# A tile of tokens ranked ahead of the others, and the order of gathers, gates and kept GELUs in a product-key expert layer on Trainium2

## The reference

```python
def peer_layer(h, w_q, sub_keys, u_tab, v_tab):      # T = 512, D = 1024
    q = (hf @ w_q).reshape(T, PEER_HEADS, 2, PEER_DQ // 2)          # 8 heads, 2 halves of 128
    s = jnp.einsum('thpd,hpnd->thpn', q, sub_keys)                  # 128 keys per half
    sc, idx = lax.top_k(s, PEER_TOPK)                               # 16 of 128
    cand = (sc[:, :, 0, :, None] + sc[:, :, 1, None, :])            # 16 x 16 sums
    cidx = (idx[:, :, 0, :, None] * PEER_NKEYS + idx[:, :, 1, None, :])
    top_sc, pos = lax.top_k(cand, PEER_TOPK)                        # 16 of 256
    eidx = jnp.take_along_axis(cidx, pos, axis=-1)                  # of 16384 experts
    gate = jax.nn.softmax(top_sc, axis=-1)
    act = gelu(einsum('thkd,td->thk', u_tab[eidx], h))
    return einsum('thk,thkd->td', gate * act, v_tab[eidx])
```

## Time and profile before

| | |
|---|---|
| median of 3 runs | 3418.14 us |
| the profiled execution | 3415.01 us, its span 3413.2 us |
| TensorE busy | 3213.3 us (94%), granted clock 0.981 as a mean |
| VectorE, ScalarE, GpSimd busy | 2236.4, 1360.5, 1723.1 us |
| DMA | 587.55 MB, mean 172 GB/s |
| up stage with its gate runs | about 820 to 1481 us of the span |
| down stage | about 1481 to 2063 us |

### The profile page before, as it was taken

How to read it: one execution, slowest core, us unless ns; L and a number is a source line. 1 busy time by engine, 2 the same in 40 slices (tenths; PEclk the granted TensorE clock), 3 DMA queues, 4 the chain that set the end, 5 groups by cost and what they waited for, 6 DMA issues and landing times.

```text
span 3413.2 us, 46478 instructions
## 1 busy us (share of the span) xinstructions
PE 3213.3 (94%) x16195; PEld 2774.4 (81%) x16195; DVE 2236.4 (66%) x4113; ACT 1360.5 (40%) x1999; POOL 1723.1 (50%) x922
## 2 busy tenths in 40 slices
PE   6999999989999999979999999898999999899998
PEld 4787787779999999979999998756888886478886
DVE  5787898769968677646666645286854332857553
ACT  4555432333454544434444443365322223632221
POOL 2222343434767667657787754662444443034443
PEclk8999999999999999989999999999999999999999
DMA  5434422223689797999999953211222232122222
GB/s 208 156 119 162 150 93 80 93 86 112 209 294 333 249 338 247 325 346 337 343 350 356 335 181 108 85 54 48 94 98 99 95 107 102 48 68 99 98 94 87
DMA packets 190046, 587.55 MB, mean 172 GB/s; under 512 B 19585, under 2 KB 52737, under 8 KB 189601
## 3 DMA queue, kind: packets, MB, share of 16 engines
q1 hardware_dynamic: 83936, 303.08, 25.5%
q10 hardware_dynamic: 69092, 148.25, 12.0%
q0 software_dynamic: 36864, 134.23, 11.8%
HBM read 532.92 MB, written 67.24 MB: 176 GB/s over the span
## 4 chain that ended last, share of the span: by engine, by line
PE 66%; DVE 13%; DMA 8%; issue 5%; ACT 3%; POOL 3%; ACTq 0%; DVEq 0%; SPq 0%; POOLq 0%
PE ps L417 19%; PE ps L419 19%; PE ps L418 19%; DMA ring<-panels 6%; POOL ring_r L2201 3%; PE ps L653 2%; DMA arena<-u_rows,arena 2%; PE ps L781 2%; DVE ps L1781 1%; PE ps L516 1%; ACT high_w L894 1%; PE ps L770 1%; DMA arena<-v_rows,arena 1%; DVE arena L1849 1%; DVE arena L1846 1%
## 5 line engine op out<-in xcount | busy, mean ns | idle before, releaser
L2201 POOL TENSOR_TENSOR ring_r<-ring,high_w 128x1024 fp32r<-128x1024 f32 x552 | 1365.6, 2476 | 1446.1 <-ACT high_w L894 1443.9
L417 PE MATMUL ps<-uT_r,high_w 128*128 128x512 f32 (+1 forms) x2608 | 986.2, 378 | 17.1 <-POOL ring_r L2201 11.5
L419 PE MATMUL ps<-uT_r,ring_r 128*128 128x512 f32 (+1 forms) x2608 | 963.6, 369 | 0.0
L894 ACT ACTIVATE high_w<-ring 128x1024 fp32r<-128x1024 f32 x552 | 582.2, 1057 | 888.1 <-PE ps L419 645.6
L418 PE MATMUL ps<-sq_r,high_w 128*128 128x512 f32 (+1 forms) x2032 | 737.3, 363 | 0.0
L418 PE MATMUL ps<-part,high_w 128*128 128x384 f32 (+1 forms) x1840 | 664.2, 361 | 0.0
L417 PE MATMUL ps<-part,high_w 128*128 128x384 f32 (+1 forms) x1664 | 599.9, 361 | 35.8 <-POOL ring_r L2201 17.3
L419 PE MATMUL ps<-part,ring_r 128*128 128x384 f32 (+1 forms) x1664 | 595.4, 358 | 0.0
L417 PEld LDWEIGHTS ps<-uT_r,high_w 128*128 128x128 f32 x2608 | 493.6, 189 | 89.3 <-POOL ring_r L2201 14.4
L419 PEld LDWEIGHTS ps<-uT_r,ring_r 128*128 128x128 f32 x2608 | 492.7, 189 | 63.4
L418 PEld LDWEIGHTS ps<-sq_r,high_w 128*128 128x128 f32 x2032 | 384.1, 189 | 39.1 <-issue 1.0
(11 more groups left out here) (354 smaller groups left out, 4065.9 us busy)
## 6 DMA issues: line engine op xcount, KB each, us to landing
ring<-panels SPq DMA_DIRECT2D x568, 512.0 KB, 3.4
gdram<-arena ACTq DMA_DIRECT2D x48, 512.0 KB, 7.3
arena<-adram ACTq DMA_DIRECT2D x128, 192.0 KB, 4.8
...
adram<-arena ACTq DMA_DIRECT2D x102, 192.0 KB, 5.2
...
```

The lines of the kernel that those rows point to most:

```text
L417: t_.matmul(out, wh, xh[:, 0:n], start=(k == 0), stop=False)
L419: last = t_.matmul(out, wl, xh[:, 0:n], start=False, stop=(k == KT - 1))
L894: s_.activation(high_w[:, j % RING], ring[:, j % RING], ACT.Copy).then_inc(hi_ready, 1)
L2201: g_.tensor_tensor(ring_r[:, j], ring[:, j], high_w[:, j], ALU.subtract).then_inc(lo_ready, 1)
```

## The change

The diff has these parts:

1. Ranking: of each head half the gathered tile is ranked at once, and of the 48 other rankings 34 are spread over the head halves; the last 14 (`LATE`) come behind `route(0)`. The copies of all scores and indices (`sc4`, `ix4`) follow behind those, with a new semaphore `all_ranked`; GpSimd waits for it before gather 3, since `u_buf[3]` lies where scores still stand. `ranked` and `ranked_at` move to another place, and `ix_s` holds tile 3's indices.
2. Gathers: the first five stand behind low halves 13, 14, 15, 20 and 21 instead of all behind 14, with the wait for `expert_ready` behind 13; each later one stands one panel earlier (`at + 3` instead of `at + 4`).
3. Dots: none in routes 2 and 3, four in route 1 (five before), and 41, 41, 42 in the stretches (38, 38, 39 before).
4. The gated one-hot becomes a `tensor_scalar` with two scalars, slot and gate, both in SBUF (`gate_c` is a copy made once per stretch), instead of a `scalar_tensor_tensor` whose second tensor is a broadcast column in PSUM.
5. `FIRST` 28 instead of 24, `BETWEEN` 8 instead of 12: 12 panels are left behind the last stretch instead of 8. The exponentials move.
6. The GELUs of the last eight up panels stay in SBUF (`gel_kept`), without store and fetch. The down groups are rolled by one, so that this group comes first. ScalarE makes the first links of its chain ahead of up panel 127's GELU. SP loads the first gates ahead of the last four up panels and the second gates behind them. The semaphore `g_first` goes.
7. Six expert sums stand ahead of the first chain and two inside it (four and four before), and the first gathers of down rows stand three panels earlier.

```diff
-FIRST, HOT, BETWEEN = 24, 24, 12
+FIRST, HOT, BETWEEN = 28, 24, 8
...
-        dots_in_route = {1: (3, 4, 5, 6, 7), 2: (1, 3, 5, 7), 3: (1, 3, 5, 7)}
-        dots_hot = {1: 38, 2: 38, 3: 39}
+        LATE = 14
+        dots_in_route = {1: (0, 2, 4, 6)}
+        dots_hot = {1: 41, 2: 41, 3: 42}
...
-            for h in range(2):
-                sp.wait_ge(g_first[h], 16 * (DENSE_TILES - h))
-            sp.wait_ge(g_out[0], 112 * DENSE_TILES)
-            sp.wait_ge(g_last[0], 32)
-            for g in range(2):
-                sp.dma_start(gi[:, g], gdram.rearrange("a h j i t -> j (a h) (i t)")[:, :, 512 * g:512 * g + 512]).then_inc(g_in[g], 16)
+            sp.wait_ge(g_out[0], 128 * DENSE_TILES)
+            sp.wait_ge(g_out[1], 128 * (DENSE_TILES - 1))
+            first_gates(0)
+            for j in range(RING):
+                load(up_loads, j)
+            first_gates(1)
...
+                act.wait_ge(gemm_done, 8 * Q_PEER + n + 1)
+                if n >= 8 * (GROUPS - 1):
+                    s_.activation(gel_kept[n % 8], ps[:, j, 0:DENSE], ACT.Gelu).then_inc(bank_free[j], 1)
+                    high(Q_PEER + n // 8, n % 8 + 3)
+                    return
...
-            exps_behind = {8: 0, 20: 1, FIRST + HOT + 6: 2, FIRST + 2 * HOT + BETWEEN + 6: 3}
+            exps_behind = {5: 0, 22: 1, FIRST + HOT + 4: 2, FIRST + 2 * HOT + BETWEEN + 4: 3}
...
                 if n == 8 * GROUPS - 2:
                     act.wait_ge(hot_ready, 5 * 32 * DENSE_TILES)
                     for m in range(2):
                         gate_copy(m)
-            for j in range(4):
-                act.wait_ge(a_out[j], 16 * 2 * GROUPS)
-            for m in range(8):
-                if m % 2 == 0:
-                    act.wait_ge(g_last[m // 2], 32)
+                    for q in range(4):
+                        act.wait_ge(g_last[q], 32)
+                    for m in range(4):
+                        hid_top(m)
+                        gate_copy(m + 2)
+            for m in range(4, 8):
                 hid_top(m)
-                fetch(m + 4)
                 gate_copy(m + 2)
...
+            others = [(tt, hp) for hp in range(16) for tt in ORDER[1:]]
+            at_once = len(others) - LATE
             for hp in range(16):
                 ve.wait_ge(sc_sb, hp + 1)
-                for tt in ORDER:
-                    ins = best(qpeer[:, hp, tt * P:(tt + 1) * P], srep[:], ranked[:, tt, hp, :], ranked_at[:, tt, hp, :])
+                ins = rank(ORDER[0], hp)
+                for n in range(hp * at_once // 16, (hp + 1) * at_once // 16):
+                    ins = rank(*others[n])
...
-                        v_.scalar_tensor_tensor(out=gated_a[:, 4 * (n % 2) + k], in0=iota, scalar=slot_a[:, now:now + 1],
-                                                in1=ps[:, 4, 2 * P + now:2 * P + now + 1].broadcast_to([P, P]),
-                                                op0=ALU.is_equal, op1=ALU.mult).then_inc(hot_ready, 1)
+                        v_.tensor_scalar(gated_a[:, 4 * (n % 2) + k], iota, slot_a[:, now:now + 1], gate_c[:, now:now + 1],
+                                         ALU.is_equal, ALU.mult).then_inc(hot_ready, 1)
...
             route(0, ORDER[0])
+            for n in range(at_once, len(others)):
+                ins = rank(*others[n])
+            S.done(ins)
+            S.mark(v_.tensor_copy(sc4, ranked))
+            v_.tensor_copy(ix4, ranked_at).then_inc(all_ranked, 1)
+            ve.wait_ge(all_ranked, 1)
+            S.wait()
             route(1, ORDER[1])
...
-            u_behind = [14] * U_BUFS + [at + 4 for at in dot_at[:SLOTS - U_BUFS]]
-            v_behind = [8 * GROUPS - 6 + k for k in range(V_BUFS)] + [8 * GROUPS + at + 3 for at in sum_at[:SLOTS - V_BUFS]]
+            u_behind = [13, 14, 15, 20, 21] + [at + 3 for at in dot_at[:SLOTS - U_BUFS]]
+            v_behind = [8 * GROUPS - 9 + k for k in range(V_BUFS)] + [8 * GROUPS + at + 3 for at in sum_at[:SLOTS - V_BUFS]]
...
-    seq += [*up, *down]
+    seq += [*up, *np.roll(down, 1, 0)]
```

87 lines of the change are left out of this document (50 added, 37 removed).

## The result

The kernel after takes 3427.39 us (median of 20 runs, 3418.6 to 3446.2); the kernel before took 3415.35 beside it (20 runs, 3403.6 to 3433.0). The ratio is 1.0038 with a 95% interval of [1.0026, 1.0049]. So the change costs 0.4%, where I had forecast a gain of 0.4%: the time lies in my range and in the case "within 0.5%", but on the wrong side of zero.

What follows compares the result with a forecast made beforehand. TensorE bounds the kernel, so time is won only where it stands still. Losses of 11.6 + 15.4 + 12.5 + 3 + 13.6 = 56.1 us against 69.4, 13.3 less, gave 3405 us, range 3380 to 3430.

Steps and rivals of the forecast that it cites:

- within 0.5%: Whole kernel: time between 3401 and 3435 us, a difference a measurement can hardly tell from none; chance 0.47.
- To the first gate run: Start to first gate run: 11.6 us lost, before 9.3, with TensorE waiting 9.3 for route 1 and 2.3 for lower clock.
- Between the stretches: Two parts between gate stretches, now eight panels each: 15.4 us lost, before 12.1, as TensorE waits for routes 2 and 3.
- Gate stretches: Three gate stretches: 12.5 us lost (bounds 5, 28), before 21.6; earlier gathers win half, the new one-hot is hidden.
- Tail: Last up panels, now twelve: 3 us lost, before 2.8, with the first gates' load ahead of the last four panels covered.
- Seam: Last up panel to end of first down panel, plus the panel behind: 13.6 us lost (bounds 9, 24), before 23.6.
- Down stage behind that panel: Down stage, 556.9 us: same bytes per panel, taken as unchanged; a change above 5 us would break the sum.
- one-hots wait for GpSimd: Slower rival, gate steps: one-hots wait for low halves, deciding from 1.5 us per step; 3448 us, chance 0.13.
- The cover holds: Faster rival: routes of 37 to 38 us start before the last gate run, late gathers vanish; 3383 us, chance 0.37.
- The seam stays: No-change rival, seam: early chain waits for a weight panel behind a gates' load; 23.6 us lost, 3415 us, chance 0.12.

Runs made afterwards that it cites:

- e1: The kernel after with the old one-hot again (gate column read from PSUM), all else kept: 3419.48 us, ratio 1.0001.
- e2: The kernel after with its new one-hot reading the row of numbers it compares with from a copy in PSUM: 3416.45 us, ratio 1.0000.
- e3: The kernel after with 3 late rankings behind route 0 instead of 14: 3427.86 us, ratio 1.0035.
- e5: The kernel after with the one-hot's row in PSUM, 8 late rankings instead of 14 and the first exponential behind panel 8 instead of 5: 3413.49 us, ratio 0.9991.
- e6: The kernel after with the one-hot's row in PSUM and the chain's first four links behind up panel 127's GELU: 3416.55 us, ratio 1.0007.

## Why the prediction was wrong

What bounds the kernel was read rightly: TensorE's stops make the time, and the account of before gives the same sum by my own cut (69.0 up to the panel behind the seam, 69.4 predicted). For after I forecast 56.1; it was 74.9. I had forecast 0.4% less time and it became 0.4% more. Two steps failed: the routes' start against the last gate run, and the new one-hot put down as hidden. The terms:

- **To the first gate run: 11.6 forecast, 10.1 measured.** Its steps held. Route 0 started at 830.2 (828.1 forecast), the first gather came at 872.6 (870.2), route 1 started at 898.3 (895.3) and was ready at 942.5 (942). The stop for five gathers is gone. The exponential held ScalarE to 850.9 (848.5) and stopped TensorE 3.5 us (3); what it took was gone from the stop ahead of the transposes, 3.3 us where I had named 5 to 10.
- **Between the stretches: 15.4 forecast, 25.3 measured.** This is the first term that failed, and in it the start of the route. I took -1.5 us against the last gate run, between -3.4 and +2; it was +2.1 both times. The length was about right: 41.3 and 43.6, forecast 41.2. With those, my own working gives 2.1 + 41.3 - 34.2 = 9.2 and 2.1 + 43.6 - 34.2 = 11.5 us of standing still. The views of TensorE's waits in the two gaps have:

```profile
PEld ps L674 <- DVE slot L1940: 9.3, 1, 9.3
```
```profile
PEld ps L674 <- DVE slot L1940: 11.6, 1, 11.6
```

  The arithmetic was sound, the start was not. Earlier gathers pull it ahead, to -2.9 and -2.7, when they are the only edit. I took 1.7 us off for denser dots, a mean; at the end of a stretch it is a whole panel, the last dot's gather stands where it stood, and the start is +3.3 and +2.8 with the packing alone and +3.8 and +1.6 in after without long one-hots. With the start late, eight panels are too few: with twelve again the same routes cost 0.1 and 0.4.
- **Gate stretches: 12.5 forecast, 21.3 measured.** The second term that failed. I had put the new one-hot at 0.2 us and hidden. Its shortest is 0.33, and it cost 10.5 us of the 21.3 (10.8 with the old one-hot), and by the ratios of the times 13 in all. The earlier gathers did what was said (10.8 here, 7.8 alone).
- **Tail: 3 forecast, 5.5 measured.** TensorE stopped twice for low halves. The first stop, 2.1 us at 1456.7, comes before the first gates' load, behind 9 us in which ScalarE issues the last eight stores. The second, 1.3 us at 1481.4, is the one that I had held covered: the first up panel that SP loads behind the first gates (issued at 1468.92) lands 10.1 us later, and ScalarE waits 5.51 us for it:

```profile
1479.09 1.06 ACT L907 ACTIVATE high_w<-ring 128x1024 fp32r<-128x1024 f32 x1 [5.51 <-DMA ring<-panels]
```

- **Seam: 13.6 forecast, 12.0 and 0.8 for the panel behind it measured.** Right in size, in part by luck: the early links, on which I had built it, are worth nothing. The first low part was out 1.5 us after TensorE's end, not 0.2 ahead, since ScalarE waited 2.85 and 1.81 us for the first two down panels ahead of the chain; the links behind it kept the pace that I took (1.6 without a sum, 2.1 with one).
- **Down stage behind that panel: unchanged forecast, 3.8 more measured** (24.6 - 0.8 against 22.2 - 2.2 in before). Five kernels with the same code there (e1, e2, e3, e5, e6) lose 19.6 to 29.4 in that column, so this difference is not shown to be the change's.

The differences are 9.9 + 8.8 + 2.5 - 1.5 - 0.8 = 18.9 of the 18.8 between 56.1 and 74.9. With the down stage's 3.8 that is about the 22 us by which the forecast missed.

Of the rivals, *one-hots wait for GpSimd* named the mechanism, and I gave it 0.13. Its sign, a mean above 0.5 us, came (0.574). What made me rank it low was its threshold: it should cost nothing below 1.5 us of waiting per step. The waiting was (574 - 336) x 4 = 0.95 us per step, below it, and cost 10.5 us in this kernel and 28 in the kernel before. The error is that I compared means. VectorE's slack, 4.01 us less about 3, is there in every step; the waiting is not 0.95 in each, but 3 us in some and nothing in others, and those few exceed the slack: TensorE waited 13 times for them, 2.1 us at most. I had written that a low half is met halfway on average, 0.9 us; the view of the line shows up to 3.16 - 0.33 = 2.8. The cost in the kernel before, on the other hand, was 28 us, of the order of that rival's 43; late gathers may have used up the slack there, which is not shown. *The cover holds* needed routes of 37 to 38 us that start ahead of the last gate run; they took 41.3 and 43.6 and started behind it. No route in any run waited less than 3.6 us, so the 37 to 38 were never reached. *The seam stays* fell.

The prediction's sentence on the Trainium skill (SBUF — State Buffer, Who interferes with whom) said that by its rule the one-hot would wait where the old one didn't. The rows of before that agreed with it (712 in the middle for a 128 x 512 `tensor_scalar`, 353 at most for the old one-hot) were before me, and I ranked them below an average. For the one-hot they were right; the gaps between the stretches they don't touch.
